# Near scores of a dilated attention packed into two places: a residue's tile of 512 columns instead of 768

## The reference

```python
DIL_GROUPS = ((128, 1), (512, 4), (2048, 16))      # window, dilation
for g, (window, dil) in enumerate(DIL_GROUPS):
    o_g, lse_g = _dilated_group(q[g], k[g], v[g], table_g, dil, window // dil)
# in a group: queries and keys of the same token residue mod dil, in blocks of 128,
off = qi + span - kj                               # a query sees its block and the one before
valid = (off >= 0) & (off <= span)
s = q @ k * 64 ** -0.5 + bias[bucket(off * dil)]   # masked where not valid
o = softmax(s) @ v;  lse = max + log(sum)
alpha = softmax(stack(lses));  o_dil = sum(alpha * outs)
```

## Time and profile before

| | |
|---|---|
| time, median of 3 runs | 3141.98 us (3140.96 to 3144.56) |
| the profiled execution's own time | 3144.81 us |
| its span, first to last instruction | 3143.0 us |
| TensorE matmul (PE) | 3122.0 us, 99% |
| VectorE (DVE) | 1523.5 us, 48% |
| ScalarE (ACT) | 1106.8 us, 35% |
| GpSimd (POOL) | 253.3 us, 8% |
| DMA queue of the loads | 30.2% of 16 engines |
| granted TensorE clock | 0.997 of full speed |

### The profile page before, as it was taken

How to read it: one execution, slowest core, us unless ns; L and a number is a source line. 1 busy time by engine, 2 the same in 40 slices (tenths; PEclk the granted TensorE clock), 3 DMA queues, 4 the chain that set the end, 5 groups by cost and what they waited for, 6 DMA issues and landing times.

```text
span 3143.0 us, 35801 instructions
## 1 busy us (share of the span) xinstructions
PE 3122.0 (99%) x14366; PEld 2535.4 (81%) x14366; DVE 1523.5 (48%) x2328; ACT 1106.8 (35%) x1552; POOL 253.3 (8%) x223
## 2 busy tenths in 40 slices
PE   9999999999999999999999999999999999999998
PEld 7888887788888888888877788888888877888887
DVE  6434435555443444344455555434556444564352
ACT  4223335333322333223344334223456433332222
POOL 0000103102000010000031021000200001110001
PEclk9999999999999999999999999999999999999999
DMA  4323322223433233333322233332322333333332
GB/s 148 100 95 94 131 91 68 74 81 94 140 95 98 91 100 101 94 100 112 91 73 75 70 99 113 95 98 91 117 96 86 96 106 98 98 100 94 98 97 74
DMA packets 92228, 304.11 MB, mean 97 GB/s; under 512 B 10320, under 2 KB 16592, under 8 KB 91484
## 3 DMA queue, kind: packets, MB, share of 16 engines
q1 hardware_dynamic: 92064, 301.83, 30.2%
HBM read 299.64 MB, written 5.29 MB: 97 GB/s over the span
## 4 chain that ended last, share of the span: by engine, by line
PE 98%; DVE 1%; ACT 0%; DMA 0%; issue 0%; SPq 0%; POOL 0%; POOLq 0%; DVEq 0%; ACTq 0%
PE bank L1623 92%; PE score_ps L1456 1%; PE out_ps L1489 1%; PE turn_ps L1467 1%; PE out_ps L1508 1%; PE score_ps L1498 1%; PE score_ps L1530 1%; PE turn_ps L1476 0%; PE out_ps L1542 0%; PE score_ps L1573 0%; PE turn_ps L1405 0%; DMA xT<-x_in 0%; PE out_ps L1561 0%; PE turn_ps L1387 0%; PE score_ps L1551 0%
## 5 line engine op out<-in xcount | busy, mean ns | idle before, releaser
L2041 DVE TENSOR_TENSOR w_lo<-raw,w_hi 128x1024 fp32r<-128x1024 f32 (+1 forms) x548 | 676.0, 1234 | 1203.6 <-ACT w_hi L1655 1202.8
L1623 PE MATMUL bank<-in_hi,w_hi 128*128 128x512 f32 x2704 | 1079.0, 399 | 2.0 <-DVE in_lo L2047 1.2
L1623 PE MATMUL bank<-in_hi,w_lo 128*128 128x512 f32 x2704 | 1055.4, 390 | 0.0
L1623 PE MATMUL bank<-in_lo,w_hi 128*128 128x512 f32 x2704 | 1054.0, 390 | 0.0
L1655 ACT ACTIVATE w_hi<-raw 128x1024 fp32r<-128x1024 f32 (+1 forms) x548 | 568.0, 1037 | 1123.5 <-PE bank L1623 1113.1
L1623 PEld LDWEIGHTS bank<-in_hi,w_hi 128*128 128x128 f32 x2704 | 508.5, 188 | 125.2 <-issue 19.9
L1623 PEld LDWEIGHTS bank<-in_hi,w_lo 128*128 128x128 f32 x2704 | 507.9, 188 | 108.8
L1623 PEld LDWEIGHTS bank<-in_lo,w_hi 128*128 128x128 f32 x2704 | 508.6, 188 | 103.6 <-issue 2.4
L1623 PE MATMUL bank<-hid_hi,w_hi 128*128 128x512 f32 x960 | 373.4, 389 | 0.0
L1623 PE MATMUL bank<-hid_lo,w_hi 128*128 128x512 f32 x960 | 373.4, 389 | 0.0
L1623 PE MATMUL bank<-hid_hi,w_lo 128*128 128x512 f32 x960 | 373.4, 389 | 0.0
(11 more groups left out here) (338 smaller groups left out, 2605.6 us busy)
## 6 DMA issues: line engine op xcount, KB each, us to landing
raw<-w_ffn_in SPq DMA_DIRECT2D x175, 512.0 KB, 3.5
raw<-w_mix SPq DMA_DIRECT2D x90, 512.0 KB, 3.5
raw<-w_ffn_out SPq DMA_DIRECT2D x80, 512.0 KB, 3.5
raw<-w_mixb SPq DMA_DIRECT2D x58, 512.0 KB, 3.6
raw<-w_mlp_in SPq DMA_DIRECT2D x32, 512.0 KB, 3.5
raw<-w_mlp_out SPq DMA_DIRECT2D x32, 512.0 KB, 3.5
raw<-w_w_out SPq DMA_DIRECT2D x16, 512.0 KB, 3.5
raw<-w_ffn_out SPq DMA_DIRECT2D x16, 256.0 KB, 2.6
```

The source lines that it names most:

```text
L1623: mm = pe.matmul(ps, lhs, rhs, start=first and step == 0, stop=last and step == 2, skip_group_check=True)
L2041: dve.tensor_tensor(w_lo[:, i % SPLIT, cut], raw[:, i % RAW, cut], w_hi[:, i % SPLIT, cut].bitcast(F32), ALU.subtract).then_inc(S_["lo_spl ...
```

## The change

The near scores (group 0) get two places of 128 columns instead of four blocks. Place 0 holds the even key block that a query reaches (block 0 for queries 0 to 63, block 2 for the rest), place 1 the odd one (block 1 for queries 0 to 95, block 3 for the rest). A tile then has 512 columns: two near places, and groups 1 and 2. It fits one bank and turns in one slot of four blocks; tiles alternate between the two banks of scores. The fillers fall from 50 to 34, and the rate from 1.9 to 1.3.

- The scores are seven products of 128 moving columns instead of three: near ones for 64, 64, 64, 32 and 32 queries, and groups 1 and 2 for 128 queries between them.
- The values are groups 1 and 2 in full, and then four near products of 64, 64, 64 and 32 moving columns, for each of two heads.
- The bias tile takes six DMAs instead of three.

```diff
+NEAR_KEYS = ((0, 0, 64, 0), (0, 64, 128, 2), (P, 0, 64, 1), (P, 64, 96, 1), (P, 96, 128, 3))
+NEAR_BIAS = ((0, 0, 64, 0), (0, 64, 128, 2), (P, 0, 96, 1), (P, 96, 128, 3))
+NEAR_VALUES = ((0, 0, 64, 0), (0, 64, 128, 2), (P, 32, 96, 1), (P, 96, 128, 3))
 
 
 def pairs(first, count):
...
+                       b=n % 2, score=self.score[n % 2].take())
         it["q_at"] = max(self.vals[k, (g * GH + h) // 2] for k in ("dq", "dk") for g in range(3))
         it["qk"] = self.add("scores")
         self.softmax(it)
-        for s in it["score"]:
-            s.over_at("top", it["top"])
+        it["score"].over_at("top", it["top"])
         it["bias"].over_at("top", it["top"])
         self.vals["dil", n] = it
 
-    def dil_turn(self, n, at, blocks):
+    def dil_turn(self, n):
         p = self.vals["dil", n]
-        it = self.item("turn", p=p["p"], ring="p2", p_ready=p["p_ready"], blocks=blocks, at=at, pt_ring="pt2")
-        if at == 0:
-            self.pt2_place = self.pt2.take()
-        it["pt"], it["turn"] = self.pt2_place, self.turn.take()
+        it = self.item("turn", p=p["p"], ring="p2", p_ready=p["p_ready"], blocks=TT, at=0, pt_ring="pt2")
+        it["pt"], it["turn"] = self.pt2.take(), self.turn.take()
         it["mm"], it["copied"] = self.add("turned"), self.add("turn_copied")
         p["p"].over_at("turned", it["mm"])
...
             if 0 <= n - 1 < GH * DIL:
-                self.filler.append(lambda n=n: self.dil_turn(n - 1, 0, 4))
-                self.filler.append(lambda n=n: self.dil_turn(n - 1, 4 * P, 2))
-        self.rate = 1.9
+                self.filler.append(lambda n=n: self.dil_turn(n - 1))
+        self.rate = 1.3
         self.tmp.grow(-MORE_TMP)
 
...
                     sp.wait_ge(S_["bias_moved"], it["laid"])
                 b = bias[it["b"].b]
-                parts = [(0, wide[h, 0:P * WIDE].rearrange("(j y) -> j y", j=P)[:, S - 1 - r_:2 * S - 1 - r_])]
-                parts += [(S + i * P, near[i * GH + h, 0:P * NEAR].rearrange("(j y) -> j y", j=P)[:, P - 1:2 * P - 1])
-                          for i in range(2)]
-                for at, src in parts:
-                    sp.dma_start(b[:, at:at + src.shape[1]], src).then_inc(S_[f"bias_tile_loaded_{it['n'] % 2}"], 16)
+                rows = wide[h, 0:P * WIDE].rearrange("(j y) -> j y", j=P)
+                for at, q0, q1, block in NEAR_BIAS:
+                    key = S - 1 - r_ + block * P
+                    sp.dma_start(b[q0:q1, at:at + P],
+                                 rows[q0:q1, key:key + P]).then_inc(S_[f"bias_tile_loaded_{it['n'] % 2}"], 16)
+                for i in range(2):
+                    src = near[i * GH + h, 0:P * NEAR].rearrange("(j y) -> j y", j=P)[:, P - 1:2 * P - 1]
+                    sp.dma_start(tok(2 + i, b), src).then_inc(S_[f"bias_tile_loaded_{it['n'] % 2}"], 16)
 
             def work(it):
...
                 h, r_ = it["h"], it["r"]
                 pe.wait_ge(S_["dve_evict"], it["q_at"])
-                for place in it["score"]:
-                    if place.over:
-                        pe.wait_ge(S_[place.over[0]], place.over[1])
-                for g, (at, width) in enumerate(((0, S), (S, P), (S + P, P))):
+                if it["score"].over:
+                    pe.wait_ge(S_[it["score"].over[0]], it["score"].over[1])
+
+                def near_keys(at, q0, q1, block):
+                    j, base = head_at(0, h)
+                    return pe.matmul(score[it["b"]][q0:q1, at:at + P], dq[j][base:base + GD, r_ * P + q0:r_ * P + q1],
+                                     tok(block, dk[j][base:base + GD, :]), start=True, stop=True, skip_group_check=True)
+
+                def residue_keys(g):
                     j, base = head_at(g, h)
-                    base = GD - base if g else base
-                    q = tok(r_, dq[j][base:base + GD, :])
-                    k = dk[j][base:base + GD, :] if g == 0 else tok(r_, dk[j][base:base + GD, :])
-                    mm = pe.matmul(score_ps[:, at:at + width], q, k, start=True, stop=True, skip_group_check=True)
-                mm.then_inc(S_["scores"], 1)
+                    rows = slice(GD - base, 2 * GD - base)
+                    return pe.matmul(tok(g + 1, score[it["b"]]), tok(r_, dq[j][rows, :]), tok(r_, dk[j][rows, :]),
+                                     start=True, stop=True, skip_group_check=True)
+
+                near_keys(*NEAR_KEYS[0])
+                residue_keys(1)
+                near_keys(*NEAR_KEYS[1])
+                near_keys(*NEAR_KEYS[2])
+                residue_keys(2)
+                near_keys(*NEAR_KEYS[3])
+                near_keys(*NEAR_KEYS[4]).then_inc(S_["scores"], 1)
 
             def dil_values(it):
...
-                for b in range(6):
+
+                def values(k, v, at, q0, q1, **flags):
+                    return pe.matmul(out_ps[GD * k:GD * k + GD, r_ * P + q0:r_ * P + q1],
+                                     v[:, (h + k) * GD:(h + k + 1) * GD],
+                                     turned_dil[it["pt"][k].b][:, at + q0:at + q1], skip_group_check=True, **flags)
+
+                for g in (1, 2):
                     for k in range(2):
-                        v = dv[:, b, 0] if b < TT else dv[:, r_, b - TT + 1]
-                        mm = pe.matmul(out_ps[GD * k:GD * k + GD, r_ * P:(r_ + 1) * P], v[:, (h + k) * GD:(h + k + 1) * GD],
-                                       turned_dil(it["pt"][k].b, b * P, P), start=b == 0, stop=b == 5, skip_group_check=True)
+                        values(k, dv[:, r_, g], (g + 1) * P, 0, P, start=g == 1, stop=False)
+                for at, q0, q1, block in NEAR_VALUES:
+                    for k in range(2):
+                        mm = values(k, dv[:, block, 0], at, q0, q1, start=False, stop=at > 0)
                 mm.then_inc(S_["valued"], 1)
 
...
-                    softmax(it, p, p[:, 0:768], 1.0, 768)
+                    softmax(it, p, p[:, 0:S], 1.0, S)
                 elif kind == "dil_values" and it["split"]:
                     act.wait_ge(S_["valued"], it["mm"])
...
                 elif kind == "dil_scores":
-                    dve.wait_ge(S_[f"bias_tile_loaded_{it['n'] % 2}"], 48 * (it["n"] // 2 + 1))
-                    softmax_biased(it, p2[it["p"].b], 768, score_ps[:, 0:768], bias[it["bias"].b])
+                    dve.wait_ge(S_[f"bias_tile_loaded_{it['n'] % 2}"], 16 * 6 * (it["n"] // 2 + 1))
+                    softmax_biased(it, p2[it["p"].b], S, score[it["b"]], bias[it["bias"].b][:, 0:S])
                 elif kind == "dil_values" and it["split"]:
                     dve.wait_ge(S_["dil_hi"], it["split"]["hi"])
```

More of the change, by code:

```diff
@@ L760, in dil_scores @@
         it = self.item("dil_scores", h=h, r=r, n=n, bias=self.vals["bias", n], p=self.p2.take(),
-                       score=[s.take() for s in self.score])
+                       b=n % 2, score=self.score[n % 2].take())
         it["q_at"] = max(self.vals[k, (g * GH + h) // 2] for k in ("dq", "dk") for g in range(3))
@@ L1176, in build @@
              ("more_tmp", [P, MORE_TMP, S], f)],
-            [("gap_14", [P, 47, S], f), ("gap_15", [P, 256], f), ("pt_2c", [P, 256], f), ("gap_16", [P, 4, S], f),
+            [("gap_14", [P, 47, S], f), ("gap_15", [P, S], f), ("gap_16", [P, 4, S], f),
              ("pt_2b", [P, S], f)],
@@ L1253, in build @@
         P_RING, PT_RING = {"p1": p1, "p2": p2}, {"pt1": pt1}
[L1255 to L1258, removed]
+        turned_dil = [pt2[:, 0:S], m["pt_2b"][:]]
         def sums_of(it):
@@ L1853, in work @@
                     if it["pt_ring"] == "pt2":
-                        to = turned_dil(it["pt"].b, it["at"], n)
+                        to = turned_dil[it["pt"].b][:, 0:n]
                     else:
```

## The result

The changed kernel takes 3148.01 us (median of 19 runs, 3146.08 to 3149.92) against 3142.73 us of the kernel before (19 runs): a ratio of 1.0016, with a 95% interval of 1.0010 to 1.0023. It is slower by 5.3 us, clear of noise, and less than the 0.2% that the forecast called a difference.

What follows compares the result with a forecast made beforehand. TensorE's own sequence was taken to bound the kernel; 14.1 - 3.8 - 3.4 - 0.7 = +6.2 us on the median of 3141.98 gave 3148.2 us (+0.20%), range 3126 to 3152.

Steps and rivals of the forecast that it cites:

- Scores: Seven score products on TensorE with four inner shape switches: 1.93 us against 1.05, +0.88 a tile, +14.1 us for 16.
- The price of a change of shape: On TensorE, each switch of array shape costs 0.08 to 0.10 us of emptying, taken as 0.09, then a bare load.
- the last load: In the scores' last near pair on TensorE, a weight load was counted as 0.055 us.
- Values: Eight value slots on TensorE: near products take eight short steps of 0.056 us, 0.42 less a slot, -3.4 us.
- Turns: The turn of two blocks goes, 0.24 us in each of 16 tiles on TensorE: -3.8 us.
- The wait: One turn's wait for ScalarE's copy of the turned dv falls by about 0.7 us: -0.7 (0 to -1.4).
- Work beside it: VectorE's add-and-maximum, exp and scale fall by a third, on engines TensorE does not wait for: worth nothing.
- added issuing on SP: Three more DMAs a tile at 0.43 us each, 1.3 us ahead of the weight load: hidden, at most 21 us without cover.
- Faster: Rival for the scores: row halves overlap in one bank, scores give -6.6 us, total 3127.5 us; chance 0.22.
- in between: Rival for the scores: no emptying, but row halves take turns in one bank, +3.0 us, total 3137.1 us; chance 0.17.
- The slower one: Rival for the scores: near pairs do not run side by side, +7.0 us more, total 3155.2 us; chance 0.08.

Runs made afterwards that it cites:

- the order: Changed kernel with the five near score products first, then groups 1 and 2: 3141.35 us, ratio 0.9999 to the kernel before.
- two-bank runs: Changed kernel, same order and shapes, with near scores in one bank and groups 1 and 2 in another: 3148.23 us, ratio 1.0018 to the kernel before.
- the DMA run: Changed kernel with each of the four near DMAs of a bias tile cut into four of 32 columns, 18 a tile: 3155.33 us.
- the quarters: Changed kernel with near scores as eight products of 32 queries, then groups 1 and 2, all in one bank: 3137.36 us, ratio 0.9984 to the kernel before.

## Why the prediction was right

**Scores, +14.1 forecast, +13.6 measured.** The price of a change of shape was taken from rows where only the columns change, 128*128 to 128*64; it held for shapes of 64 rows within 0.01 us. The one term mis-sized is the last load (32 columns, 0.03 for 0.055). The row halves don't overlap when their shapes differ, although they share no part of the array; the order and the two-bank runs separate this from the bank. It is what the Trainium skill, TensorEngine Tiling (Array Packing), Key Properties, says, and here it is shown without overlapping tiles. The rule of the Trainium skill, TensorEngine Tiling (Array Packing), Restrictions and Gotchas, that different row tiles cannot use one PSUM bank at the same time, played no part: with the shapes as they are the halves never run together.

**Values, -3.4 forecast, -3.5 measured.** Steps of 64 columns are 0.058 us. The two of 32 columns start 0.03 apart, though each comes with a load of 64 columns, for which I had set a bound of 0.055; what follows them takes longer, so that all eight steps cost 0.44 us, 0.055 each in the mean. **Turns, -3.8 forecast, -3.6 measured**; the row's two decimals were too coarse. That a tile turns in one slot is worth almost nothing; that it has four blocks and not six is worth the 3.6. **The wait, -0.7 forecast, -0.7 measured**, by the position of the slot in its beat.

**Work beside it.** The shorter softmax, the freed bank and the added DMAs changed nothing, as forecast. For the bank a run shows it. For the other two it is read from the trace: in the stage TensorE waits only 0.7 us, for the turned dv. The forecast's 1.3 us a tile of added issuing on SP was 1.7; the DMA run puts a limit to it.

**The rivals.** Faster and in between needed overlap or no emptying; both are excluded by the gaps between the stretches. The slower one needed near products that run in turn; the two products of each x4 group take the time of one, and the quarters go four at a time.

The sum was +6.2 and the runs show +5.3. The scores came out 0.5 us cheaper, and the two small waits that went (0.2 us) weren't in the sum. The forecast lay at the edge of 0.2% and the result just inside it: which side it fell on was luck, the mechanism and its price weren't.

## What to carry to other kernels

In these runs small products in different rows or columns of the array were free beside each other only while all had one shape of rows and columns. Each change of shape cost 0.09 us and a bare load, so group products by shape, or cut all to the smallest shape: sixteen products of 64*32 took 0.60 us where seven of three shapes took 1.90. Before work is packed to save columns, count the changes of shape that the packing adds; here four of them ate more than the packing saved.

## What the runs showed of the hardware that had not been expected

Sixty-four instructions of TensorE (32 loads and 32 products) were issued and run in 0.60 us, eight products side by side at 0.109 us a step, so that issue didn't bind. And a bias tile cut into eighteen DMAs filled SP: an issue took 0.43 to 0.58 us, and from 2482 to 2656 us SP waited for 0.8 us in all. A sum over a wider window hides this: from 2470 to 2690 us SP still shows 44.6 us of waiting, nearly all of it ahead of the first tile and behind the last.
